# Attention in a hybrid decoder layer: the value products of two heads put side by side in the array, with transposed outputs

## The chip, the cores and the metric

The kernel runs on one core of one Trainium2 chip. The metric is the device time of one execution in microseconds (us). Engines are named as in the profile: PE (matrix multiply; PEld is its weight load), DVE (vector), ACT (scalar activations), POOL (GpSimd) and SP (issues most DMAs).

## The reference

One step of a one-layer hybrid decoder for a prompt of 1024 tokens behind 16 learned meta tokens (T = 1040 rows) and eight single-token samples, all in fp32. The layer has a state-space head group and a latent attention head group; both feed an output projection and a feed-forward part. The change touches only the causal attention of the prompt, with 8 heads, query and key width 96, value width 64, in query blocks of 128:

```python
s = jnp.einsum('bqhd,bkhd->bhqk', qb, kp).astype(jnp.float32) * ATTN_SCALE
s = jnp.where(kpos[None, :] <= qpos[:, None], s, -jnp.inf)
p = jax.nn.softmax(s, axis=-1)
return jnp.einsum('bhqk,bkhd->bqhd', p.astype(vp.dtype), vp)
```

The last einsum is the value product.

## The kernel before

The program is five blocks one after the other: the tiles block (projections, state-space scan, queries, keys, values into DRAM), the attention block (`attention_block`, this case), the samples block (paged attention of the eight samples), the mixing block and the feed-forward block. A block starts when every engine has finished the one before.

The attention block works on **units**. A unit is a query tile t of 128 rows with some of its heads: all 8 heads at t = 0, four at t = 1, two at t = 2 and 3, one from t = 4 on. Together 43 units, each head of which attends to t + 1 key blocks of 128. Two **tail units**, for the last 16 rows of four heads each, stand at places 39 and 43, so K = 45. All engines walk n from 0 up in the same order, written out by hand:

- PE, at step n: `turn(n - 2)` transposes the probabilities of unit n - 2 block by block into PSUM banks 6 (first half of the blocks) and 7 (second half) (L1216); `scores(n)` multiplies queries and keys into three PSUM banks, 0 to 2 or 3 to 5 by the parity of n (L1188, tail units L1200); `values(n - 2)` multiplies (L1228, tail units L1235).
- DVE, at step n: `copy_first(n - 2)` copies bank 6 into SBUF (`pt[0]`, L1119), `maximum(n)` adds the mask (L1106), takes the row maximum (L1113) and scales it (L1114); after the last unit of a tile, `finish` divides the tile's output by the row sums (L1133, L1134).
- ACT, at step n: `copy_second(n - 2)` copies bank 7 into `pt[1]` (L1166), `exps(n)` computes the exponentials with their row sums, one instruction for each head (L1155, tail units L1159).
- SP loads k, q and v tile by tile (L1059 to L1061), then the pages of the first two samples for the next block, then stores the attention output (L1068, L1073).

In `values`, the transposed probabilities (128 keys x 128 queries) are the weights of the matmul and 64 columns of v stream past them; the output has the queries on the 128 partitions and 64 columns for a head. All heads of a tile gather in one bank, 2 or 5 by the parity of t:

```python
ins = pe.matmul(ps[:, o_bank(t), h * VD:(h + 1) * VD], pt[g][:, c, :], v[:, b, h * VD:(h + 1) * VD],
                start=(b == 0), stop=(b == t))
```

One fp32 `matmul` of the program is two pairs of LDWEIGHTS and MATMUL in the trace, which the rows call records; a fp32 transpose is one pair. So 288 matmuls of `values` are 576 records. The tail units put four heads side by side, each in its own 32 columns of the array, at partitions 0, 32, 64 and 96 of the output (L1200, L1235); the samples block does the same at L1796 and L1799.

Of the kernel before, what the change touches and what calls it, by code (L numbers as in the profile page):

```python
# [24 lines left out]
ALU = mybir.AluOpType  # L25
# [944 lines left out]
def attention_block(nc, s, pages):  # L970
# [19 lines left out]
    done_order = sorted([(last_unit[t], t) for t in range(NT)] + [(n, NT) for n in tails])  # L990
# [7 lines left out]
    pt = [sb(f"pt{i}", [P, 4, P]) for i in range(2)]  # L998
# [11 lines left out]
    loaded = [sem(f"loaded{t}") for t in range(6)]  # L1010
    load_of = [0, 1, 2, 3, 4] + [5] * (NT - 4)
    loads = [3 * 16 * load_of.count(i) for i in range(6)]
# [4 lines left out]
    o_ready, att_done, att_stored = sem("o_ready"), sem("att_done"), sem("att_stored")  # L1017
    dve_steps = Steps(sem("dve_steps"), "attention dve")
    pool_steps = Steps(sem("pool_steps"), "attention pool")
    block = ctx.enter_context(nc.Block())  # L1020

    def o_bank(t):
        return 2 if t % 2 else 5

    TAIL_BANK = 5
# [14 lines left out]
    def outputs(n):  # L1040

        return [m for m, _ in done_order].index(n) + 1
# [8 lines left out]
    def output_done(n):  # L1051
        return is_tail(n) or n == last_unit[units[n][0]]
# [25 lines left out]
    def _(pool):  # L1078
# [4 lines left out]
        pool.affine_select(out=mask[:, :], in_=mask[:, :], compare_op=ALU.is_ge, fill=NEG,  # L1083
                           base=0, pattern=[[-1, P]], channel_multiplier=1).then_inc(consts, 1)
# [9 lines left out]
    def _(dve):  # L1094
# [21 lines left out]
        def copy_first(n):  # L1116
            dve.wait_ge(turned[0], first_turns(n))
            w = len(blocks_of(n)[0]) * P if not is_tail(n) else 4 * P
            dve.tensor_copy(pt[0][:, :, :].rearrange("p b r -> p (b r)")[:, 0:w], ps[:, 6, 0:w]).then_inc(copied[0], 1)  # L1119
# [5 lines left out]
        def finish(n):  # L1125
            dve.wait_ge(o_ready, n + 1)
            if not is_tail(n):
                t = units[n][0]
                l, o, dst = lsum[t][:, :], by_head(ps[:, o_bank(t), :], VD), by_head(att[:, t, :], VD)
            else:  # L1130
                u = tails.index(n)
                l, o, dst = ltail[:, u:u + 1], ps[:, TAIL_BANK, VD:2 * VD].unsqueeze(1), atail[:, u:u + 1, :]
# [1368 lines left out]
```

## Time and profile before

| | us |
|---|---|
| median of 3 runs | 2163.18 (2162.9 to 2163.27) |
| profiled execution, its own time | 2163.01 |
| span of the profiled execution | 2161.3 |
| attention block on PE, first scores to last value product | 477.4 to 653.5 |
| PE busy over the span | 2010.4 (93%) |
| DVE busy | 1192.9 (55%) |
| ACT busy | 624.0 (29%) |
| POOL busy | 634.9 (29%) |

The profile is one execution. Starts are counted in us from the start of the span. The duration of a matmul record holds its way through the pipeline, so records that follow each other overlap in time; what a stream costs is read from the distance between starts. In rows that merge several records, the first number is the start of the first one and x is their count.

### The profile page before, as it was taken

The page shows a single profiled execution, that of the slowest core. Times are in us where ns is not written, and L with a number is a line of the kernel's source. Part 1 is how long each engine was busy: PE and PEld are TensorE (multiplying, and loading weights), DVE is VectorE, ACT ScalarE, POOL GpSimd, SP SyncE. Part 2 cuts the span into 40 slices and gives each one's busy share as a digit, 9 for nine tenths or more (in the row PEclk, how much of TensorE's full clock was granted, in tenths as well). Part 3 has the DMA queues.
Part 4 walks back from the last instruction along what each step waited for, and adds up shares of the span by engine and source line. Part 5 has one row for each costly group of instructions (what it writes and reads, how often), then busy time and mean ns, then how long its engine had stood idle before and what let it go on. Part 6 is the DMA issues. An engine that isn't in the chain of part 4 may idle for free. (4 is left out here: it accounts for less than half of the span.)

```text
span 2161.3 us, 35037 instructions
## 1 busy us (share of the span) xinstructions
PE 2010.4 (93%) x12543; PEld 1636.4 (76%) x12543; DVE 1192.9 (55%) x1992; ACT 624.0 (29%) x1292; POOL 634.9 (29%) x586
## 2 busy tenths in 40 slices
PE   8999999759997999999999659799999999999998
PEld 4566666438876777777777438699999999999997
DVE  4567666736653766665666435354444444544444
ACT  2233332224433444443545222121111111211110
POOL 1334344330003533333323133242232322333211
PEclk9999999869997999999999879899999999999999
DMA  5111111147411012322223051212210122102201
GB/s 219 21 38 37 37 42 37 47 97 160 105 48 38 20 29 67 84 72 68 59 70 90 12 186 39 59 40 59 59 40 20 56 58 58 39 19 58 58 19 79
DMA packets 180683, 132.00 MB, mean 61 GB/s; under 512 B 61757, under 2 KB 165486, under 8 KB 180438
## 3 DMA queue, kind: packets, MB, share of 16 engines
q1 hardware_dynamic: 177190, 129.37, 21.1%
q0 software_dynamic: 144, 1.08, 0.2%
q8 instruction: 71, 1.16, 0.2%
q10 hardware_dynamic: 3232, 0.01, 0.1%
q14 instruction: 46, 0.38, 0.1%
HBM read 110.81 MB, written 19.65 MB: 60 GB/s over the span
## 5 line engine op out<-in xcount | busy, mean ns | idle before, releaser
L2399 PE MATMUL f_ps<-nT_hi,f_gu_hi 128*128 128x344 f32 x1056 | 338.3, 320 | 6.7 <-POOL f_gu_lo L2271 6.7
L2399 PE MATMUL f_ps<-nT_hi,f_gu_lo 128*128 128x344 f32 x1056 | 337.7, 320 | 0.0
L2399 PE MATMUL f_ps<-nT_lo,f_gu_hi 128*128 128x344 f32 x1056 | 337.4, 320 | 0.0
L1507 POOL TENSOR_TENSOR s_b_latT<-s_b_latT_hi,s_b_latT_lo 128x1024 f32<-128x1024 f32 x64 | 153.5, 2399 | 348.8 <-DVE s_b_latT_lo L1561 348.8
L1628 DVE TENSOR_REDUCE s_b_ssq<-s_b_ksq 128x8 f32<-128x512 f32 x256 | 172.8, 685 | 120.1 <-ACT s_b_ksq L1426 118.0
L1426 ACT ACTIVATE s_b_ksq<-s_ps 128x512 f32<-128x512 f32 x256 | 153.6, 600 | 215.5 <-PE s_ps L1779 171.6
L1779 PE MATMUL s_ps<-s_b_wk_hi,s_b_latT_hi 128*128 128x512 f32 x512 | 208.2, 407 | 7.0 <-ACT s_b_ksq L1426 7.0
L2399 PEld LDWEIGHTS f_ps<-nT_hi,f_gu_hi 128*128 128x128 f32 x1056 | 199.1, 189 | 7.5 <-POOL f_gu_lo L2271 7.1
L1779 PE MATMUL s_ps<-s_b_wk_lo,s_b_latT_hi 128*128 128x512 f32 x512 | 201.5, 394 | 0.0
L1779 PE MATMUL s_ps<-s_b_wk_hi,s_b_latT_lo 128*128 128x512 f32 x512 | 201.2, 393 | 0.0
L2399 PEld LDWEIGHTS f_ps<-nT_hi,f_gu_lo 128*128 128x128 f32 x1056 | 199.0, 188 | 0.0
L2399 PEld LDWEIGHTS f_ps<-nT_lo,f_gu_hi 128*128 128x128 f32 x1056 | 198.6, 188 | 0.4
L2361 DVE TENSOR_TENSOR h<-f_ps,h 128x1024 f32<-128x1024 f32 x88 | 107.8, 1225 | 144.2 <-PE f_ps L2428 144.2
L2372 DVE TENSOR_SCALAR f_e<-f_e 128x344 f32<-128x344 f32 x66 | 26.0, 394 | 239.2 <-ACT f_e L2327 239.2
L2373 DVE RECIPROCAL f_e<-f_e 128x344 f32<-128x344 f32 x66 | 152.0, 2303 | 2.2
L2286 POOL TENSOR_TENSOR f_hid_lo<-f_e,f_hid_hi 128x344 fp32r<-128x344 f32 x66 | 61.6, 933 | 281.4 <-ACT f_hid_hi L2335 281.4
L2428 PE MATMUL f_ps<-f_wd_hi,f_hid_hi 128*128 128x512 f32 x352 | 139.6, 397 | 0.2 <-issue 0.2
L2428 PE MATMUL f_ps<-f_wd_hi,f_hid_lo 128*128 128x512 f32 x352 | 138.7, 394 | 0.0
L2428 PE MATMUL f_ps<-f_wd_lo,f_hid_hi 128*128 128x512 f32 x352 | 138.7, 394 | 0.0
L2271 POOL TENSOR_TENSOR f_gu_lo<-gu_raw,f_gu_hi 128x1024 fp32r<-128x1024 f32 x44 | 105.7, 2423 | 87.1 <-ACT f_gu_hi L2312 86.6
L768 PE MATMUL t_ps<-t_w_in,t_xT 128*128 128x512 f32 (+2 forms) x384 | 130.8, 497 | 0.0
L1779 PEld LDWEIGHTS s_ps<-s_b_wk_hi,s_b_latT_hi 128*128 128x128 f32 x512 | 97.4, 190 | 29.4 <-ACT s_b_ksq L1426 10.0
(367 smaller groups left out, 3615.2 us busy)
## 6 DMA issues: line engine op xcount, KB each, us to landing
p_latn<-in_cache_kv_latent SPq DMA_DIRECT2D x256, 128.0 KB, 2.0
gu_raw<-in_w_gate SPq DMA_DIRECT2D x22, 512.0 KB, 4.0
gu_raw<-in_w_up SPq DMA_DIRECT2D x22, 512.0 KB, 5.4
f_wd_raw<-in_w_down SPq DMA_DIRECT2D x11, 1024.0 KB, 5.0
t_w_in<-in_w_in SPq DMA_DIRECT2D x8, 980.0 KB, 13.3
t_x<-in_x_prompt SPq DMA_DIRECT2D x8, 512.0 KB, 5.6
p_krn<-in_cache_k_rope SPq DMA_DIRECT2D x256, 16.0 KB, 1.8
h<-in_w_out SPq DMA_DIRECT2D x8, 512.0 KB, 9.0
```

Source lines behind the costliest of these rows:

```text
L768: ins = pe.matmul(dst, l, r, start=(n == 0), stop=(n == len(lhsT) - 1))
L1426: out(act.activation(ksq[j % 2][:, :], ps[:, 3 + j % 2, :], ACT.Square, scale=QK ** -0.5), "sq_done")
L1507: out(pool.tensor_tensor(out=flat(latT), in0=flat(latT_hi).bitcast(F32), in1=flat(latT_lo).bitcast(F32), op=ALU.add), "sum_done")
L1628: out(dve.tensor_reduce(ssq[p][:, GP * g + j, :], by_head(ksq[j % 2][:, :], NOPE), AXX, ALU.add), "red_done")
L1779: ins = pe.matmul(ps[:, 3 + j % 2, :], l[g % 2][:, c, j, :], w[:, c, :], start=(c == 0 and l is latT_hi and w is wk_hi), stop=(c == 1 and ...
L2271: out(pool.tensor_tensor(out=gu_lo[p][:, j, :, :], in0=gu_raw[:, j, :, :], in1=gu_hi[p][:, j, :, :].bitcast(F32), op=ALU.subtract), "gu_lo ...
L2286: out(pool.tensor_tensor(out=hid_lo[q][:, fi, cols], in0=e[c][:, :], in1=hid_hi[q][:, fi, cols].bitcast(F32), op=ALU.subtract), "hid_lo_done")
L2361: out(dve.tensor_tensor(out=rows_, in0=ps[0:R, bank:bank + 2, :], in1=rows_, op=ALU.add), "h_added")
L2372: dve_steps(dve, dve.tensor_scalar(e[c][:, :], e[c][:, :], 1.0, None, ALU.add))
L2373: dve_steps(dve, dve.reciprocal(e[c][:, :], e[c][:, :]))
L2399: ins = pe.matmul(ps[:, bank + j, 0:W], w[fi][:, j, k, :], x[:, k, cols], start=(k == 0 and w is gu_hi and x is nT_hi), stop=(k == KD - 1 ...
L2428: ins = pe.matmul(ps[0:R, bank + c, :], x[q][:, fi, col:col + R], w[:, fi, cols], start=(fi == 0 and w is wd_hi and x is hid_hi), stop=(fi ...
```

## The change

The value product is turned round. The 64 columns of v of one head become the weights, the transposed probabilities (128 columns) stream past them, and the output has the value dimension on the partitions and the queries in the free dimension. Two heads share the array: the even one in columns 0 to 63 (output partitions 0 to 63), the odd one in columns 64 to 127 (partitions 64 to 127); their matmuls are issued in turn, key block by key block, each after a wait for the copy of its block.

- Units are gathered into **jobs**: up to t = 3 a unit is a job; from t = 4 on two successive units (two heads) are one. There are 27 jobs: 1, 2, 4, 4, and four for each of t = 4 to 7. `values(j)` runs on PE at the step of the job's last unit + 2, after `scores(n)`, into bank 2, whatever the tile. It waits until ACT has read the job before out of that bank.
- ACT copies the turned output of the job from bank 2 to SBUF (`keep_turned_output`, one of four buffers `oT`), at the start of its step last + 3, ahead of `copy_second` and `exps`.
- PE turns it back, one 128 x 128 transpose for each head pair (32 in all), at step last + 5, between `turn` and `scores`, into bank 5 (`back`).
- DVE divides by the row sums for each job, no longer for each tile, from bank 5, at step last + 5, ahead of `maximum`.
- `pt` has three slots for each half: two for the units of a job and one for the tail units.
- The tail units keep their products in 32-column groups, now into bank 2. A tail unit's scores still wait for bank 5 to be free, now on the division of the last job turned back, which at both tail units is that of the same step.
- The loads of tiles 3 and 4 share a semaphore, and PE waits for the identity matrix instead of for the mask (not shown).

```diff
-    done_order = sorted([(last_unit[t], t) for t in range(NT)] + [(n, NT) for n in tails])
+    jobs = []
+    for t in range(NT):
+        own = [n for n in range(K) if units[n][0] == t]
+        step = 1 if len(units[own[0]][1]) > 1 else 2
+        jobs += [own[i:i + step] for i in range(0, len(own), step)]
+    ending = {job[-1]: j for j, job in enumerate(jobs)}
+    BACK = 5
+    done_order = sorted([(job[-1] + BACK, job[-1]) for job in jobs] + [(n + 3, n) for n in tails])
...
-    pt = [sb(f"pt{i}", [P, 4, P]) for i in range(2)]
+    pt = [[sb(f"pt{i}{j}", [P, 4, P]) for j in range(3)] for i in range(2)]
+    oT = [sb(f"oT{i}", [P, H // 2, P]) for i in range(4)]
...
-    load_of = [0, 1, 2, 3, 4] + [5] * (NT - 4)
...
+    load_of = [0, 1, 2, 3, 3] + [4] * (NT - 4)
...
-    def o_bank(t):
-        return 2 if t % 2 else 5
...
+    O_BANK, BACK_BANK = 2, 5
...
+    def pt_slot(n):
+
+        if is_tail(n):
+            return 2
+        return [job.index(n) for job in jobs if n in job][0]
...
+        def finish(j):
+            t, heads = units[jobs[j][0]][0], heads_of(j)
+            l = lsum[t][:, heads[0]:heads[0] + len(heads)]
             dve_steps(dve, dve.reciprocal(l, l))
-            dve.tensor_tensor(out=dst, in0=o, in1=bc(l, VD, 2), op=ALU.mult).then_inc(att_done, 1)
-
-        dve.wait_ge(consts, 2)
-        for n in range(K + 3):
+            dve.wait_ge(back_ready, j + 1)
+            cols = slice(heads[0] * VD, (heads[-1] + 1) * VD)
+            dve.tensor_tensor(out=by_head(att[:, t, cols], VD), in0=by_head(ps[:, BACK_BANK, 0:len(heads) * VD], VD),
+                              in1=bc(l, VD, 2), op=ALU.mult).then_inc(att_done, 1)
+
+        def finish_tail(n):
+            u = tails.index(n)
+            l = ltail[:, u:u + 1]
+            dve_steps(dve, dve.reciprocal(l, l))
+            dve.wait_ge(o_ready, outputs_before(n) + 1)
+            dve.tensor_scalar(atail[:, u, :], ps[:, O_BANK, 0:VD], l, None, ALU.mult).then_inc(att_done, 1)
...
+        for n in range(K + BACK):
             if 2 <= n < K + 2:
                 copy_first(n - 2)
+            if n - 3 in tails:
+                finish_tail(n - 3)
+            if n - BACK in ending:
+                finish(ending[n - BACK])
             if n < K:
                 maximum(n)
             if n - 2 in tails:
                 copy_last(n - 2)
-            if n >= 3 and output_done(n - 3):
-                finish(n - 3)
...
+        def keep_turned_output(j):
+            w = len(heads_of(j)) // 2
+            act.wait_ge(o_ready, outputs_before(jobs[j][-1]) + 1)
+            if j >= 4:
+                act.wait_ge(back_ready, j - 3)
+            act.activation(oT[j % 4][:, 0:w, :], ps[:, O_BANK, 0:w * P].rearrange("p (w r) -> p w r", r=P),
+                           ACT.Copy).then_inc(oT_copied, 1)
+
+        for n in range(K + 3):
+            if n - 3 in ending:
+                keep_turned_output(ending[n - 3])
+            if 2 <= n < K + 2:
                 copy_second(n - 2)
             if n < K:
...
-                pe.wait_ge(att_done, outputs(tails[u - 1] if u else last_unit[NT - 2]))
+                backs = [job[-1] for job in jobs if job[-1] + BACK <= n]
+                pe.wait_ge(att_done, outputs(backs[-1]))
...
+        def values(j):
+            if j >= 1:
+                pe.wait_ge(oT_copied, j)
+            for m in tails:
+                if m + 2 < jobs[j][-1] + 2 and (j == 0 or jobs[j - 1][-1] < m):
+                    pe.wait_ge(att_done, outputs(m))
+            for w in range(len(heads_of(j)) // 2):
+                pair = heads_of(j)[2 * w:2 * w + 2]
+                blocks = {h: [] for h in pair}
+                for n in jobs[j]:
+                    for g in range(2):
+                        for c, (i, h, b) in enumerate(blocks_of(n)[g]):
+                            if h in pair:
+                                blocks[h].append((n, g, c))
+                t = units[jobs[j][0]][0]
+                for b in range(t + 1):
+                    for i, h in enumerate(pair):
+                        n, g, c = blocks[h][b]
+                        pe.wait_ge(copied[g], first_turns(n) if g == 0 else n + 1)
+                        ins = pe.matmul(ps[i * VD:(i + 1) * VD, O_BANK, w * P:(w + 1) * P], v[:, b, h * VD:(h + 1) * VD],
+                                        pt[g][pt_slot(n)][:, c, :], start=(b == 0), stop=(b == t))
             ins.then_inc(o_ready, 1)
 
-        pe.wait_ge(consts, 1)
-        for n in range(K + 2):
-            if n >= 2:
+        def back(j):
+            pe.wait_ge(oT_copied, j + 1)
+            if j >= 1:
+                pe.wait_ge(att_done, outputs(jobs[j - 1][-1]))
+            for w in range(len(heads_of(j)) // 2):
+                ins = pe.transpose(ps[:, BACK_BANK, w * P:(w + 1) * P], oT[j % 4][:, w, :], ident[:, :])
+            ins.then_inc(back_ready, 1)
+
+        def tail_values(n):
+            u = tails.index(n)
+
+            pe.wait_ge(oT_copied, sum(job[-1] < n for job in jobs))
...
+        pe.wait_ge(consts, 2)
+        for n in range(K + BACK):
+            if 2 <= n < K + 2:
                 turn(n - 2)
+            if n - BACK in ending:
+                back(ending[n - BACK])
             if n < K:
                 scores(n)
-            if n >= 2:
-                values(n - 2)
+            if n - 2 in ending:
+                values(ending[n - 2])
+            if n - 2 in tails:
+                tail_values(n - 2)
```

`tail_values` goes on as the old tail branch did, into bank 2.

## Rows read from the trace of the kernel before

**Rows 1.** The page: the chain that ended last, by engine.
```profile
PE 35%; POOL 0%; issue 0%; DVE 0%; ACT 0%
```

**Rows 2.** Busy time of PE, PEld, DVE, ACT, POOL, 500 to 620 us, attention block.
```profile
500.00:620.00 120.00, 119.96 (x805) 96.83 (x804) 77.28 (x151) 50.05 (x117) 0.00 (x0) 1.00 0.43 111
```

**Rows 3.** PE in order of time, eight-block units (start us, us, engine, what).
```profile
613.59 1.90 PE L1228 MATMUL a_ps<-a_v,a_pt 128*128 128x64 f32 x16
615.32 1.04 PE L1216 MATMUL a_ps<-a_ident,a_prob 128*128 128x128 f32 x8
616.20 1.88 PE L1188 MATMUL a_ps<-a_k,a_q 96*128 96x512 f32 x4
617.92 1.90 PE L1228 MATMUL a_ps<-a_v,a_pt 128*128 128x64 f32 x16
```

**Rows 4.** PE in order of time, a six-block unit.
```profile
555.88 1.45 PE L1228 MATMUL a_ps<-a_v,a_pt 128*128 128x64 f32 x12
557.17 0.82 PE L1216 MATMUL a_ps<-a_ident,a_prob 128*128 128x128 f32 x6
557.83 1.46 PE L1188 MATMUL a_ps<-a_k,a_q 96*128 96x512 f32 x4
```

**Rows 5.** SP's queue: last stores of the attention output, first load after them.
```profile
616.40 38.39 SPq L1068 DMA_DIRECT2D s_att<-a_att  x2
654.83 3.67 SPq L1073 DMA_DIRECT2D s_att<-a_atail  x8
659.92 0.52 SPq L1346 DMA_DIRECT2D s_b_h<-in_state_ssm  x1
```

**Rows 6.** PE's groups by form, 477 to 654 us: the value matmuls.
```profile
L1228 PE MATMUL a_ps<-a_v,a_pt 128*128 128x64 f32 x576 | 69.7, 272 | 0.4 <-DVE a_pt L1119 0.3
```

**Rows 7.** PE in order of time in the samples block: 128, 32, 128 columns.
```profile
686.89 0.39 PE L1779 MATMUL s_ps<-s_b_wk_lo,s_b_latT_hi 128*128 128x512 f32 x1
687.12 0.39 PE L1779 MATMUL s_ps<-s_b_wk_hi,s_b_latT_lo 128*128 128x512 f32 x1
687.44 0.65 PE L1796 MATMUL s_ps<-s_b_latT,s_b_qab 128*32 128x128 f32 x16
687.90 0.40 PE L1799 MATMUL s_ps<-s_b_krT,s_b_qab 128*32 128x128 f32 x8
688.23 1.09 PE L1730 MATMUL s_ps<-s_b_ident,p_latn 128*128 128x128 f32 x8
689.16 0.27 PE L1733 MATMUL s_ps<-s_b_ident,p_krn 128*128 128x128 f32 x1
```

**Rows 8.** PE in order of time, a tail unit: matmuls in 32-column groups.
```profile
631.50 1.10 PE L1235 MATMUL a_ps<-a_v,a_pt 128*32 128x64 f32 x64
633.48 0.31 PE L1235 MATMUL a_ps<-a_v,a_ptl 16*32 16x64 f32 x8 [0.88 <-DVE a_ptl L1123]
```

**Rows 9.** ACT's groups by form in the block, and a 128-wide copy of the next.
```profile
L1166 ACT ACTIVATE a_pt<-a_ps 128x512 f32<-128x512 f32 x17 | 10.1, 594 | 2.8 <-PE a_ps L1216 2.8
L1166 ACT ACTIVATE a_pt<-a_ps 128x384 f32<-128x384 f32 x20 | 9.7, 483 | 0.0
L1155 ACT ACTIVATE a_prob<-a_ps,a_nmx 128x1024 f32<-128x1024 f32 x8 | 8.9, 1116 | 21.4 <-DVE a_nmx L1114 21.4
...
688.37 0.28 ACT L1428 ACTIVATE s_b_scs<-s_ps 128x128 f32<-128x128 f32 x1 [0.22 <-PE s_ps L1799]
```

**Rows 10.** DVE's groups by form in the block: division and reciprocal.
```profile
L1134 DVE TENSOR_TENSOR a_att<-a_ps,a_lsum 128x512 f32<-128x512 f32 x8 | 5.5, 692 | 0.3
...
L1133 DVE RECIPROCAL a_lsum<-a_lsum 128x8 f32<-128x8 f32 x8 | 1.6, 195 | 1.8 <-PE a_ps L1228 1.8
```

**Rows 11.** DVE, then ACT, in order of time, beside the unit of rows 4.
```profile
556.08 0.30 DVE L1106 TENSOR_TENSOR a_ps<-a_ps,a_mask 128x128 f32<-128x128 f32 x1 [1.06 <-PE a_ps L1188]
556.42 0.96 DVE L1113 TENSOR_REDUCE a_mx<-a_ps 128x1 f32<-128x768 f32 x1
...
557.60 0.90 ACT L1155 ACTIVATE a_prob<-a_ps,a_nmx 128x768 f32<-128x768 f32 x1 [1.64 <-DVE a_nmx L1114]
```

More of the change, by code:

```diff
@@ L1008, in attention_block @@
     ident = sb("ident", [P, P])
-    loaded = [sem(f"loaded{t}") for t in range(6)]
-    load_of = [0, 1, 2, 3, 4] + [5] * (NT - 4)
-    loads = [3 * 16 * load_of.count(i) for i in range(6)]
+    loaded = [sem(f"loaded{t}") for t in range(5)]
+    load_of = [0, 1, 2, 3, 3] + [4] * (NT - 4)
+    loads = [3 * 16 * load_of.count(i) for i in range(5)]
     consts, scores_ready, max_ready, exp_done = [
@@ L1017, in attention_block, with heads_of @@
     o_ready, att_done, att_stored = sem("o_ready"), sem("att_done"), sem("att_stored")
+    oT_copied, back_ready = sem("oT_copied"), sem("back_ready")
     dve_steps = Steps(sem("dve_steps"), "attention dve")
-    pool_steps = Steps(sem("pool_steps"), "attention pool")
+    pool_steps = Steps(consts, "attention constants")
     block = ctx.enter_context(nc.Block())
-    def o_bank(t):
-        return 2 if t % 2 else 5
-    TAIL_BANK = 5
+    O_BANK, BACK_BANK = 2, 5
+    def heads_of(j):
+        return [h for n in jobs[j] for h in units[n][1]]
+    def pt_slot(n):
+        if is_tail(n):
+            return 2
+        return [job.index(n) for job in jobs if n in job][0]
     def places(n):
@@ L1040, in outputs, with outputs_before @@
     def outputs(n):
-        return [m for m, _ in done_order].index(n) + 1
+        return [m for _, m in done_order].index(n) + 1
+    def outputs_before(n):
+        return sum(job[-1] < n for job in jobs) + sum(m < n for m in tails)
     def first_turns(n):
@@ L1049, in is_tail @@
         return units[n][0] == NT
-    def output_done(n):
-        return is_tail(n) or n == last_unit[units[n][0]]
     @block.sync
@@ L1082, in _ @@
         pool_steps(pool, pool.memset(mask[:, :], 0.0))
-        pool.affine_select(out=mask[:, :], in_=mask[:, :], compare_op=ALU.is_ge, fill=NEG,
-                           base=0, pattern=[[-1, P]], channel_multiplier=1).then_inc(consts, 1)
+        pool_steps(pool, pool.affine_select(out=mask[:, :], in_=mask[:, :], compare_op=ALU.is_ge, fill=NEG,
+                                            base=0, pattern=[[-1, P]], channel_multiplier=1))
         pool_steps(pool, pool.memset(tmask[:, :], 0.0))
@@ new lines, in back, with weigh @@
+        def back(j):
[8 more added lines that the diff above has]
+            pe.wait_ge(oT_copied, sum(job[-1] < n for job in jobs))
+            def weigh(b, w, src):
+                for i in range(HT):
+                    h = u * HT + i
+                    ins = pe.matmul(ps[i * QT:(i + 1) * QT, O_BANK, 0:VD], src[0:w, i * QT:(i + 1) * QT],
+                                    v[0:w, b, h * VD:(h + 1) * VD], start=(b == 0), stop=(b == NT))
+                return ins
+            pe.wait_ge(copied[0], first_turns(n))
+            pe.transpose(ps[0:META, 6, 0:P], prob[n % 2][:, SEQ:T], ident[:, :]).then_inc(turned[0], 1)
+            for b in range(4):
+                weigh(b, P, pt[0][2][:, b, :])
+            pe.wait_ge(copied[1], n + 1)
+            for b in range(4):
+                weigh(4 + b, P, pt[1][2][:, b, :])
+            pe.wait_ge(copied[0], first_turns(n) + 1)
+            weigh(NT, META, ptl).then_inc(o_ready, 1)
```

43 lines of the change are left out of this document (3 added, 40 removed).

## The prediction

> **What bounds the kernel now.** I read the page first. Its chain that ended last lies on PE for the part it reaches back over [rows 1], and that part is the feed-forward block, which the change leaves alone. So the question is whether the attention block ends sooner, and whether what follows moves with it. The busy table of the block's steady part comes next: PE 119.96 of 120 us, DVE 77, ACT 50, at a granted clock of 1.00, that is 2.4 GHz [rows 2]. PE has no gap to fill; time leaves here only if PE is given less to do, and only as long as DVE and ACT still arrive in time. PE's order of time then gives the price of each piece by the distance between starts: for eight key blocks, values 1.73 us (16 records), transposes 0.88, scores 1.72, period 4.33 [rows 3]; for six, values 1.29 and transposes 0.66 [rows 4], with scores of 6 x 0.215 a period of 3.24. So a key block of one head costs 0.216 of values, 0.11 of transposes and 0.215 of scores.
>
> At the end of the block SP issues the last small stores, and 1.4 us after the last of them the next block's first load starts [rows 5]. Since a block starts when the one before is done, a shorter attention block should pass its gain on whole. The page loads for the next block are in SP's queue ahead of the stores; a store that stands behind them goes out at 616.40 [rows 5], 37 us before the block's end, so they cost nothing up to a gain of that size.
>
> **What goes.** 576 records of values [rows 6], two for each of 288 matmuls: 288 x 0.216 = 62.2 us. A record streams only 64 columns but loads 128 columns of weights, and its distance of 0.108 is the same as that of a transpose with 128 columns and 128 weights (0.11) [rows 3]. The weights set the old price.
>
> **What comes in its place.** 288 matmuls that stream 128 columns past 64 weight columns, two at a time if the column groups overlap. The trace has no two 64-column groups side by side. The nearest rows have four 32-column groups. In the samples block 16 records of 128 columns take 0.46 us from start to the next line's start: four waves of four, 0.115 each [rows 7]. In the tail unit 64 records of 64 columns last 1.10 us with the pipeline's own 0.2 us in it [rows 8], which is 16 waves at 0.055. So groups side by side cost what one costs. At two groups I take 0.22 us for both heads' matmuls of one key block (two records each): 144 x 0.22 = 31.7 us, a gain of 30.5. Bounds: both groups one after the other, 63.4 us (a loss of 1.2); less than 31.7 can't be, as 128 columns of an fp32 record have no shorter distance in any row.
>
> The Trainium skill (TensorE: Matmul & The Clock Gate, Packing small matmuls) gives a measured 2.38x for three column groups. At that efficiency, by an estimate from its figure, two groups would give 1.59x, the new products 40 us, and the forecast would be some 8 us later. The 64 records of the tail unit speak against it: a full fourfold rate.
>
> **Switches of column width.** Before the 32-column records of rows 7 the distance is 0.32 instead of 0.23; behind them, the last two waves and the way out take 0.33 instead of 0.22, and the eight transposes after that 0.93 instead of 0.88. Together 0.09 + 0.11 + 0.05 = 0.25 us for going in and out. 27 jobs: 6.8 us. Bounds 0 and 13. The Trainium skill (TensorEngine Tiling, Key Properties) says a change of tiling mode drains the engine; the 0.25 us is this trace's size of it, and the page gives none.
>
> **Turning back.** 32 transposes at 0.11: 3.5 us on PE. ACT gets 27 copies, 24 of them 128 wide at 0.28 us [rows 9], about 8 us on an engine that is busy 42% of the time [rows 2]. DVE's 8 divisions of 512 columns with their reciprocals, 7.1 us [rows 10], become 27 smaller ones at about 0.5 (0.2 + the 0.3 that 128 columns take in rows 11), 13 us, on an engine that is busy 64%. Neither becomes the busiest. The semaphore that tiles 3 and 4 now share and the wait for the identity matrix cost nothing: PE runs without a gap from 500 us on, and all loads of both tiles were needed soon after in any case. The 288 waits ahead of single matmuls are for copies mostly long done; one in the middle of the value stream of rows 3 leaves the 16 records at 1.73 us, so I take zero, bound 288 x 0.01 = 3.
>
> **PE's sum:** -62.2 + 31.7 + 6.8 + 3.5 = **-20.2 us**, -4.0 of it up to t = 3 and -16.2 from t = 4 on.
>
> **The waits that come.** PE's slack was what covered DVE and ACT, and the products now come in one lump every second unit. Take t = 5, counted from the end of a unit's scores (555.88 in rows 4). DVE's mask and maximum and ACT's exponential follow; ACT starts it at 557.60 and is free 0.90 later [rows 11]; only then it can do `copy_second` of the unit before, 0.48 [rows 9]: 3.10 us, 3.15 with the semaphore. PE in the new order has transposes 0.66, the next scores 1.29, the way in 0.09, and seven matmuls (0.77) before it needs the second half of that unit: 2.81. It stands for about 0.35 us a pair. The same count gives 0.3 at t = 4. For eight blocks the exponential takes 1.12, the copy 0.59 [rows 9] and DVE at most 0.3 more (0.96 us for 768 columns), 3.8 us, against 0.88 + 1.72 + 0.09 + 0.99 = 3.68: 0.1 or less, and so at t = 6. Per pair, old to new with the wait: t = 4, 5.41 to 5.0; t = 5, 6.48 to 5.93; t = 6, 7.57 to 6.5; t = 7, 8.66 to 7.37. Four pairs each: -13.2 us.
>
> Up to t = 3 every unit is a job. `values` of the next one waits until ACT has emptied bank 2, and ACT does that behind two or more exponentials of the unit between: about 1.7 (DVE) + 1.2 + 0.28 = 3.2 us against 2.85 of PE work, and `copy_second` stands behind it. I take 0.3 for each of 11 jobs, 3.2 us; bounds 0 and the whole 4.0. What is left is -0.8.
>
> The tail units break the rhythm. Unit 43's scores wait for a division of the same step, which stands in DVE's queue behind the maximum of unit 42 (2.0 from the end of its scores: the 1.7 of rows 11 and 0.3), a copy (0.6, as on ACT) and its own 0.5: 3.1 us where PE arrives after 1.0, so 2.1; at unit 39 values lie between, 0.5. Unit 43's own products wait for a copy that DVE does behind the maximum of unit 44: 2.6 against 0.9, so 1.7, then 0.5 for ACT's half; the last job waits 0.5 for the tail's division, and the last transpose back 0.4 for ACT's copy. 5.7 us; bounds 2 and 9.
>
> **Sum:** -13.2 - 0.8 + 5.7 = -8.3, or -20.2 + 3.0 + 3.2 + 5.7. From the profiled execution's own 2163.0 (span 2161.3 and 1.7 around it) this is 2154.7; the median of the runs is 0.2 higher. Some waits overlap with the drain of a switch (PE stands anyway), so I say **2154.5**.
>
> **Rivals.**
> (1) *The two groups run one after the other* (slower). Place: `values`, where each matmul begins with a wait, and both passes of one head are issued before the other head's. If the other group can't start until they are through, the products cost 63.4 us instead of 62.2; with 3.5 and 6.8 and some 4 of waits (less, as PE is late itself) it is +15: **2178**. It decides at a price of 0.17 us a matmul: from there on the change loses. For: no row has two 64-column groups with a wait on each matmul. Against: the tail units issue both passes of one head, then the next, and reach the fourfold rate [rows 8]. Chance 0.09.
> (2) *The waits are hidden or small*, and the PE sum is nearly had: -15 to -20, **2146**. For: ACT and DVE are half idle. Against: the counts above are in order and leave no slack at t = 4, 5 and at the tails. Chance 0.14.
> (3) *Emptying PSUM becomes the limit.* ACT now has three jobs in a fixed order, and a late one delays `copy_second`, hence the next transposes, hence the next exponentials. If this costs 0.5 us more at each of the 16 pairs, nothing is left: **2163**. Against: at t = 7 ACT has about 2.0 us of work a unit and DVE 2.7, PE 3.6. Chance 0.09. The Trainium skill (TensorEngine Tiling, PSUM Bottleneck) states it as a rule: tiling speeds up the matmuls, not the copies.
> (4) *Forecast case*, 2148 to 2161: chance 0.68.
>
> **Numbers.** About 0.2% (4.3 us) can be told from no change. Faster by more: the forecast case up to 2159, and (2): 0.83. Within: 0.08, from (3) and the forecast's upper edge. Slower: (1), 0.09. The range 2147 to 2161 leaves out (1), half of (3) and a part of (2).
>
> **What the profile would show.** Right: MATMUL records of `values` of form 128*64 with 128 columns, starting in pairs, 16 key blocks of a pair's two heads in about 1.8 us instead of 3.5; the block ending near 645 instead of 653.5; PE idle before `values` on ACT's `pt`, and a gap of about 2 us before the second tail's scores; busy PE in 500 to 600 no longer full. Wrong: 3.5 us for the 16 (rival 1); no idle time on PE in the block (rival 2); a period of 8.6 us for two eight-block units with PE idle a sixth of it (rival 3); or the next block's start not moving with the end of attention, which no row of before excludes.

## The result and the profile after

| | before | after |
|---|---|---|
| time, median of 5 runs each, same chip | 2163.18 us (2161.58 to 2163.86) | 2172.83 us (2171.12 to 2174.62) |
| ratio after / before | | 1.0046, 95% interval 1.0031 to 1.0060 |
| profiled execution: span, own time | 2161.3, 2163.0 us | 2169.2, 2171.12 us |

The changed kernel is slower, by 9.65 us. The forecast was 2154.5 us and faster. Of all runs below one was slow, one of e6's ten with 7369.55 us, and its ratio leaves it out. The page of the changed kernel first: its totals, two of its DMA queues and the chain by engine.

```profile
PE 2000.2 (92%) x12575; PEld 1608.6 (74%) x12575; DVE 1197.6 (55%) x2030; ACT 630.0 (29%) x1319; POOL 633.8 (29%) x586
...
q8 instruction: 107, 1.75, 0.3%
...
q14 instruction: 67, 0.55, 0.1%
...
PE 35%; issue 0%; DVE 0%; POOL 0%; ACT 0%; DVEq 0%
```

The chain is still PE's [rows 1]. What a reader passes over easily are the two queues named "instruction": they bring code. In the page of before they had 71 and 46 packets.

**Where the time went** is read from the first PE instruction of each block. PE in order of time (start us, us, engine, what), before:

```profile
477.44 0.77 PE L1188 MATMUL a_ps<-a_k,a_q 96*128 96x128 f32 x2 [14.96 <-DMA a_v<-s_v]
664.58 0.64 PE L1712 MATMUL s_ps<-s_b_ident,p_wk 128*64 128x128 f32 x2 [11.12 <-POOL s_b_ones L1492]
1241.05 0.56 PE L2132 MATMUL m_ps<-m_ident,gu_raw 8*128 8x8 f32 x4 [7.36 <-DMA gu_raw<-s_att]
1396.33 0.65 PE L2399 MATMUL f_ps<-nT_hi,f_gu_hi 128*128 128x344 f32 x1 [6.68 <-POOL f_gu_lo L2271]
```

and after:

```profile
474.43 0.98 PE L1222 MATMUL a_ps<-a_k,a_q 96*128 96x128 f32 x3 [14.52 <-DMA a_v<-s_v]
657.47 0.85 PE L1773 MATMUL s_ps<-s_b_ident,p_wk 128*64 128x128 f32 x3 [10.57 <-POOL s_b_ones L1553]
1240.58 0.56 PE L2193 MATMUL m_ps<-m_ident,gu_raw 8*128 8x8 f32 x4 [8.50 <-DMA gu_raw<-s_att]
1396.61 0.66 PE L2460 MATMUL f_ps<-nT_hi,f_gu_hi 128*128 128x344 f32 x1 [6.68 <-POOL f_gu_lo L2332]
```

The differences of such rows give one line for each kernel. The last column runs to the start of PE's last instruction; 3.0 us of the first column are chance, since the tiles block is the same code in all of them (its ends scatter from 474.4 to 478.1 where nothing is put in front of attention).

| kernel | start of attention | attention | samples | mixing | feed-forward |
|---|---|---|---|---|---|
| before | 477.4 | 187.1 | 576.5 | 155.3 | 760.2 |
| after | 474.4 | 183.0 | 583.1 | 156.0 | 767.9 |
| e1: after, PE's code moved back | 486.9 | 181.4 | 573.5 | 156.1 | 760.8 |
| e2: after, ACT's moved back | 477.5 | 181.8 | 580.4 | 156.3 | 768.0 |
| e3: after, all moved back | 487.4 | 182.0 | 572.8 | 154.9 | 760.2 |
| e4: before, code moved as in after | 485.0 | 187.2 | 584.0 | 156.4 | 768.3 |
| e5: after, hidden padding | 476.8 | 181.5 | 577.2 | 156.0 | 760.8 |
| e8: e5 with the wait filled | 477.0 | 179.9 | 578.9 | 156.1 | 760.7 |
| e9: e8, all in the old places | 477.4 | 186.2 | 574.5 | 154.9 | 760.2 |
| e10: before, 56 more on PE | 477.2 | 187.3 | 577.2 | 156.6 | 760.9 |
| e11: before, 64 more | 476.1 | 187.2 | 574.0 | 156.3 | 760.9 |
| e14: before, 88 more | 478.1 | 189.2 | 575.2 | 156.8 | 765.5 |
| e13: before, 112 more | 477.0 | 191.9 | 579.6 | 156.3 | 767.9 |

Each line is one execution. Attention did get shorter: 187.1 to 183.0 us, and 181.4 to 182.0 in e1, e2, e3 and e5, which repeat it. Then 6.6 us are lost in the samples block, 0.7 in mixing and 7.7 in feed-forward, blocks in which the change edits nothing.

The chain of waits in the feed-forward block, 1560 to 1740 us, shows where. Before it is PE alone; after, once in each pass of the loop (every 139 us), PE stands. Before, then after (start us, us, what):

```profile
1560.00 43.36 PE f_ps L2399 x276
1603.36 0.99 PE f_ps L2410 x8
```

```profile
1559.88 21.69 PE f_ps L2460 x138
...
1581.66 0.53 DVE f_e L2437
1582.19 0.37 issue
1582.56 2.45 PE f_ps L2460 x14
1585.01 0.30 issue
1585.31 20.57 PE f_ps L2460 x130
```

PE's waits of the changed kernel, 1400 to 2150 us (us in total, times, longest), have two entries that before lacks:

```profile
PE f_ps L2460 <- DVE f_e L2437: 4.3, 4, 1.2
PE f_ps L2460 <- issue: 1.1, 4, 0.3
```

5.4 of the 7.7 us stand there, four times 1.35. Division (DVE) is charged although it had been done as early as in before; "issue" is the better name. By the distance from one jump back to the next, each of the four passes takes 1.6 to 2.0 us more (137.4 before, 139.0 to 139.3 after), 7.1 us together. The DMA view from 1580 to 2120 us says what PE lacks. Before, then after (queue, kind: packets, MB, share):

```profile
q1 hardware_dynamic: 31296, 23.07, 14.8%
```

```profile
q1 hardware_dynamic: 31296, 23.07, 14.9%
q8 instruction: 34, 0.56, 0.4%
```

Same data, and 34 packets of code of 16 KB that before doesn't fetch: there PE's loop is fetched once and stays. Such a packet holds 256 instructions: between the first and the last of ten fetches inside attention, the trace of before has 2306 records of PE, weight loads and waits included. Counted like this the change adds 112 records on PE, 50 on ACT and 67 on DVE, all in attention, so every later loop moves. By the compiled programs PE's feed-forward loop (1614 instructions) moves from 118 to 230 behind a border of 256.

The samples block has the same sign. PE's waits in it, before, then after:

```profile
PE s_ps L1730 <- issue: 6.4, 2, 3.3
```

```profile
PE s_ps L1791 <- issue: 10.8, 4, 3.4
...
PE s_ps L1791 <- DMA p_krn<-in_cache_k_rope: 2.8, 3, 1.1
```

The four kernels that have PE's code in the changed place (after, e2, e4, e13) stand 9.7 to 10.8 us on "issue" there, in four pieces; all others 6.2 to 6.9 us in two.

**Inside attention** the rows that answer to rows 2 to 4 and 8. Busy time by engine, 500 to 620 us and from there to 654 (which holds 7 us behind attention's end), as in rows 2:

```profile
500.00:620.00 120.00, 118.85 (x894) 80.45 (x893) 84.16 (x193) 58.92 (x148) 0.00 (x0) 1.00 0.39 102
620.00:654.00 34.00, 21.28 (x286) 15.31 (x284) 12.14 (x29) 9.23 (x16) 0.75 (x5) 0.85 0.03 10
```

PE in order of time, six-block units (rows 4 before), eight-block units and the tails:

```profile
553.98 1.97 PE L1273 MATMUL a_ps<-a_pt,a_v 128*64 128x128 f32 x24
555.88 0.88 PE L1251 MATMUL a_ps<-a_ident,a_prob 128*128 128x128 f32 x6
556.59 0.27 PE L1282 MATMUL a_ps<-a_ident,a_oT 128*128 128x128 f32 x1
...
560.03 1.97 PE L1273 MATMUL a_ps<-a_pt,a_v 128*64 128x128 f32 x24
...
606.87 2.13 PE L1273 MATMUL a_ps<-a_pt,a_v 128*64 128x128 f32 x32
608.93 1.09 PE L1251 MATMUL a_ps<-a_ident,a_prob 128*128 128x128 f32 x8
...
610.86 1.97 PE L1235 MATMUL a_ps<-a_k,a_q 96*32 96x512 f32 x24 [0.73 <-DVE a_att L1148]
...
628.33 2.31 PE L1235 MATMUL a_ps<-a_k,a_q 96*32 96x512 f32 x24 [1.94 <-DVE a_att L1148]
630.57 3.24 PE L1273 MATMUL a_ps<-a_pt,a_v 128*64 128x128 f32 x32
...
639.09 0.27 PE L1298 MATMUL a_ps<-a_ident,a_prob 128*16 128x128 f32 x1 [1.65 <-DVE a_pt L1136]
...
640.12 1.08 PE L1293 MATMUL a_ps<-a_v,a_pt 128*32 128x64 f32 x32 [0.18 <-ACT a_pt L1190]
...
641.50 1.97 PE L1251 MATMUL a_ps<-a_ident,a_prob 128*128 128x128 f32 x8
...
644.23 1.97 PE L1273 MATMUL a_ps<-a_pt,a_v 128*64 128x128 f32 x32 [0.59 <-issue]
646.57 0.33 PE L1282 MATMUL a_ps<-a_ident,a_oT 128*128 128x128 f32 x1 [0.37 <-ACT a_oT L1197]
```

Eight key blocks of two heads take 2.06 us from start to the next line's start (606.87 to 608.93) instead of twice 1.73 [rows 3]: the two column groups do work side by side. The same 32 records take 3.24 at 630.57, behind the longest wait. The eight transposes at 641.50 are slow too, 1.97 us instead of 1.09 at 608.93: from 641 to 643 us the granted clock is 0.50 in this execution.

### The profile page after: what moved, and what is told of

Its sections match the earlier page's. It is cut to its first block and busy times, and to the rows that moved or that the text cites. A ratio compares the mean times of both kernels' runs of the same rounds, so it can differ in the third digit from the quotient of the medians.

```text
span 2169.2 us, 35266 instructions
## 1 busy us (share of the span) xinstructions
PE 2000.2 (92%) x12575; PEld 1608.6 (74%) x12575; DVE 1197.6 (55%) x2030; ACT 630.0 (29%) x1319; POOL 633.8 (29%) x586
## 3 DMA queue, kind: packets, MB, share of 16 engines
q0 software_dynamic: 144, 1.08, 0.2%
## 5 line engine op out<-in xcount | busy, mean ns | idle before, releaser
L1622 DVE TENSOR_TENSOR s_b_latT_lo<-s_ps,s_b_latT_hi 128x512 fp32r<-128x512 f32 x128 | 82.6, 685 | 67.6 <-ACT s_b_latT_hi L1469 67.4
```

Source lines behind the costliest of these rows:

```text
L1622: out(dve.tensor_tensor(out=latT_lo[g % 2][:, :, 2 * bank:2 * bank + 2, :], in0=ps[:, bank, :].rearrange("p (c j t) -> p c j t", c=2, t=P) ...
```

## The experiments

Moving code needs instructions that do nothing. Two waits on a met semaphore become one instruction. In the first set they stand where the engine waits for attention's first data. Each set ran on a chip of its own with before beside it, so sets are compared by their ratios.

### First set: is it the place of the code?

```diff
-        pe.wait_ge(consts, 2)
+        for _ in range(289):            # e1, e3: 144 instructions on PE
+            pe.wait_ge(consts, 2)
+        for _ in range(156):            # e2, e3: 78 on ACT
+            act.wait_ge(consts, 2)
+        for _ in range(123):            # e3: 61 on DVE
+            dve.wait_ge(consts, 6)
```

(e4 has 112, 50 and 67 such instructions in the kernel before.)

**e1_after_pe.** 

> The changed kernel with 144 more instructions on PE that do nothing (waits that are already met), put where PE waits for attention's first load; they move PE's later code to the place modulo 256 instructions that it had before. Theory A (code placement: PE's feed-forward loop of 1614 instructions now lies over 8 blocks of 256 instead of 7 and is fetched again in each of its passes): the feed-forward block takes 761.9 us again instead of 769.5, the fetches of PE's queue stop inside the loop, and the kernel takes 2172.8 - 7.6 = 2165 us; the samples block stays at 563 us. Theory B (the loss behind attention comes from data: the clock, DMA traffic or SBUF places of the later blocks): no change, 2173 or slower.

**e2_after_act.** 

 Theory A (code placement): the samples block takes 555.5 us again instead of 563.3, kernel 2165 us; the feed-forward block stays at 769.5. Theory B: no change, 2173. Rival within A: the samples block's loss is due to PE's or DVE's code, then ACT's alone changes nothing, and the first kernel or the third of this set shows it.

**e3_after_all.** 

> The changed kernel with do-nothing instructions on PE (144), ACT (78) and DVE (61), so that all code behind attention lies as in the kernel before, modulo the block size of its engine. Theory A: the gain of attention comes through: 2172.8 - 7.6 - 7.8 and up to 1.9 for the mixing block = 2155.5 to 2157.5 us, which is the forecast's 2154.5 within its rounding. Theory B: 2173. If only part of the loss is placement: between.

**e4_before_all.** 

> The kernel before, its attention untouched, with do-nothing instructions in attention's head on PE (112), ACT (50) and DVE (67), which put all later code where the changed kernel has it. Theory A: it is slower by what the changed kernel lost behind attention, 7.6 + 7.8 and up to 1.9: 2178.5 to 2180.5 us, with the fetches inside the feed-forward loop as in the changed kernel. Theory B: no change, 2163.

| | median us | ratio to before (2161.99, 21 runs) |
|---|---|---|
| e1 | 2165.48 | 1.0012 (1.0003 to 1.0022) |
| e2 | 2169.33 | 1.0035 (1.0023 to 1.0048) |
| e3 | 2164.02 | 1.0012 (1.0002 to 1.0022) |
| e4 | 2184.39 | 1.0102 (1.0085 to 1.0118) |

The expectations took the blocks between other marks (samples 555.5 and 563.3, feed-forward 761.9 and 769.5 us); what counts in them is the difference.

Theory B falls: e4 has the attention of before and loses 22.4 us, 14.9 without the padding's own 7.5. Theory A holds by the blocks. With PE's code moved back (e1, e3) feed-forward takes 760.8 and 760.2 us; with ACT's alone (e2) it stays at 768.0. The samples block surprised: PE's place gives back 9.6 us (e1), ACT's alone 2.7 (e2), so the 7.8 that I had put on ACT belong mostly to PE, and e2's total missed its 2165. The totals of e3 and e4 missed because the padding was not free: attention starts 10.0 and 7.5 us later than in before. Taken off, e3 is at 2154 and e4 at 2177. That e1's total met its forecast of 2165 is luck: 9.5 us of padding (its attention starts at 486.9) hide what the samples block gave back. What one such instruction costs is seen in e1 (count, duration in ns, first and last start in us):

```profile
L1308 PEldq EVENT_SEMAPHORE  x144: 51/51/51, 471.2 to 486.7; - x144
```

They start 0.108 us apart, 15.5 us in all. In before PE waits 6.4 us for the data at this place; in e1 the padding runs over the same wait, so only the rest shows.

### Second set: padding that hides, and what is left in attention

e5 puts 52 instructions on PE behind attention's last transposes back, and 42 on ACT at the old place. e6 to e8 are e5 with one edit each:

```diff
+        for _ in range(104):            # e5, behind the loop over units
+            pe.wait_ge(oT_copied, 1)
@@ e6
-                        pe.wait_ge(copied[g], first_turns(n) if g == 0 else n + 1)
+                        need = first_turns(n) if g == 0 else n + 1
+                        if need > waited[g]:
+                            pe.wait_ge(copied[g], need)
+                            waited[g] = need
@@ e7
-            if n - 3 in ending:
-                keep_turned_output(ending[n - 3])
             if 2 <= n < K + 2:
                 copy_second(n - 2)
+            if n - 3 in ending:
+                keep_turned_output(ending[n - 3])
@@ e8, in scores() of the second tail unit, ahead of its wait for DVE
+                    for _ in range(16):
+                        pe.transpose(flat[:, lo:lo + P], ident[:, :], ident[:, :])
```

**e5_pads_hidden.** 

> The changed kernel with 52 do-nothing instructions on PE behind its last transposes back, where PE stands 11 us before the next block, and 42 on ACT in attention's head. Theory A (code placement, and the padding at PE's head cost its own 10 us in the first set): nothing is paid for the padding, attention's own gain of some 5 us is left whole: 2172.8 - 7.7 (feed-forward) - 9 (samples, as the first kernel of the first set) = 2156 us, with attention up to the next block's first PE instruction at 182 us. Rival (PE's samples loop needs the very place it had before): the samples block stays above 580 us and the kernel at 2162 to 2165.

**e6_fewer_waits.** 

> The kernel with the hidden padding, and the values' wait ahead of each single matmul kept only where the awaited value rises (the instructions and their places are the same, only the waits go). The forecast priced the 288 waits at zero, bound 3 us. If zero holds: the PE span of attention is unchanged (170.9 us within 0.3). If each costs 0.01 us: 2 to 3 us less.

**e7_copy_first.** 

> The kernel with the hidden padding, and ACT copies the second half of a unit's turned probabilities before it keeps a job's turned output, instead of after. If ACT's order is what makes PE stand within the jobs (0.23 to 0.31 us at the record 14 of the jobs of five and six key blocks): those gaps shrink by up to the copy's 0.28, some 2 us in all. If the exponential ahead of the copy sets it, as the forecast said: unchanged within 0.5 us; and the next job's start may come later, since its wait for the kept output is then served later.

**e8_fill_wait.** 

> The kernel with the hidden padding, and 16 transposes of the identity matrix (the region is written over by the scores behind them) in front of the last tail unit's wait, so that PE works in the 1.9 us in which it stood there; padding behind is shortened by as many instructions. Theory C (the granted clock fell from 2.4 to 1.2 GHz because PE stood still at the second tail unit, and the 24 scores and 32 products behind it paid 0.54 and 1.08 us): the granted clock stays at 1.00 there, the products take 1.97 instead of 3.05 us, attention ends 1.6 us sooner. Rival (the clock falls for another reason, or the transposes delay the scores by themselves): no gain, or up to 0.5 us lost.

| | median us | ratio to before (2162.05, 26 runs) | PE, first to last of attention |
|---|---|---|---|
| e5 | 2158.51 | 0.9979 (0.9970 to 0.9989) | 170.7 us |
| e6 | 2158.90 | 0.9983 (0.9973 to 0.9993) | 171.0 |
| e7 | 2158.47 | 0.9977 (0.9966 to 0.9989) | 171.5 |
| e8 | 2158.65 | 0.9976 (0.9965 to 0.9987) | 169.0 |

e5 beats both kernels: the same arithmetic as the changed kernel, some 14 us less, for nothing but places. It is 2.5 us above my 2156; the samples block took 577.2 where e1 had 573.5, and 2.2 of these 3.7 us are waits for a load of `p_krn` that e1 doesn't have. e6: the waits ahead of single matmuls cost nothing that can be seen. e7: ACT's order isn't what stops PE in the jobs of six blocks; the copy waits behind the exponential either way. In e5 ACT's exponential starts at 555.53 and the copy directly behind it at 556.43 for 0.48 us, and PE's next record starts at 556.96; in e7 the copy starts at 557.66 and PE's record at 558.19. The 0.8 us that e7 takes more on PE lie at the block's start, where its granted clock stays low for longer (0.50 from 491 to 495 us, 0.93 in e5). e8 shows the clock. PE in order of time at the second tail unit and the 20 us around it (the last columns are granted clock, DMA share, GB/s), e5:

```profile
630.19 2.51 PE L1237 MATMUL a_ps<-a_k,a_q 96*32 96x512 f32 x24 [1.94 <-DVE a_att L1148]
632.64 3.05 PE L1275 MATMUL a_ps<-a_pt,a_v 128*64 128x128 f32 x32
...
632.00:634.00 2.00, 2.00 (x26) 1.64 (x20) 1.22 (x2) 0.00 (x0) 0.00 (x0) 0.50 0.00 0
620.00:640.00 20.00, 16.48 (x179) 10.89 (x177) 10.33 (x22) 6.71 (x14) 0.00 (x0) 0.91 0.00 1
```

and e8:

```profile
628.31 1.91 PE L1233 MATMUL a_ps<-a_ident 128*128 128x128 f32 x16
630.32 1.97 PE L1240 MATMUL a_ps<-a_k,a_q 96*32 96x512 f32 x24
632.22 1.97 PE L1278 MATMUL a_ps<-a_pt,a_v 128*64 128x128 f32 x32
...
620.00:640.00 20.00, 17.36 (x222) 11.85 (x224) 11.38 (x25) 7.95 (x17) 0.00 (x0) 1.00 0.00 1
```

In e5 PE stands 1.94 us, the granted clock falls from 2.4 to 1.2 GHz (0.50 from 632 to 634 us; 0.91 is the mean over 20 us), and scores and products behind it take 0.54 and 1.08 us longer. With PE kept at work over the same wait the clock stays at 1.00, the two lines take 1.97 each, and attention is 1.7 us shorter, here and in e9, which has the same filling (168.8). Not every stand does it: PE also waits 1.65 us before 640.95 in e5, and the clock stays at 1.00. The total doesn't show the gain: the samples block of e8's profiled execution is 1.7 longer, and the medians of e5 and e8 differ by 0.14 us. Where the 1.7 us go stays open.

### Third set: old places, the border, and the order of the heads

```diff
@@ e9: e8 with 112 instructions on PE behind attention, 78 on ACT and 61 on DVE at its head
@@ e10, e11 (and e13, e14): before, behind the loop over units; 2 x 56, 2 x 64, 2 x 112, 2 x 88
+        for _ in range(2 * 56):
+            pe.wait_ge(consts, 1)
@@ e12: e5 with
-                for b in range(t + 1):
-                    for i, h in enumerate(pair):
+                for i, h in enumerate(pair):
+                    for b in range(t + 1):
```

**e9_old_places.** 

> The changed kernel with the 16 filling transposes at the second tail unit and do-nothing instructions on PE (112, behind attention's last transposes back), ACT (78) and DVE (61), so that all code behind attention lies where the kernel before has it, modulo the block size, and the padding hides. Theory A (placement) with theory C (clock): attention 179.9 us as in the kernel with the filled wait, samples 573 to 576.5, mixing 155, feed-forward 760.3: 2155 to 2157 us. Rival (a shorter attention block is partly given back by the samples block itself, as its first pages came 0.9 us nearer to those of the kernel before without any code moved): 2158 as with the two kernels with hidden padding.

**e10_before_56.** 

> The kernel before with 56 do-nothing instructions on PE behind attention's last values, where PE stands 11 us. The feed-forward loop (1614 instructions) then begins 175 behind a border of 256 and ends 3 instructions ahead of one: 7 blocks. Theory A: the feed-forward block stays at 760.3 us and is fetched once; the samples block may change by a few us, since its loop moves too. Rival (any moved code costs, by distance, not by the count of blocks): the feed-forward block takes longer here already.

**e11_before_64.** 

> The same with 64 instead of 56: the feed-forward loop begins at 183 and reaches 5 instructions into an eighth block. Theory A: the feed-forward block takes 768 us, with fetches in each pass, for 8 instructions that do nothing; the samples block as in the kernel with 56 within 1 us; so 7 to 8 us slower than that one. Rival: no difference from the kernel with 56 that can be measured.

**e12_head_by_head.** 

> The changed kernel with the hidden padding of the second set, and in the values all products of one head issued before those of the other (same instructions, same columns of the array, other order). If the two column groups work side by side only because their products stand next to each other in the queue: the 32 records of a job of eight key blocks take 3.5 to 3.9 us instead of 1.97, attention is 27 us longer or more in PE's sum (144 x 0.22 = 31.7 us twice instead of once, less the waits that this hides), kernel some 2185 us: this is what the forecast's first rival would have cost. If the array looks further ahead: unchanged, 2158.5.

e9: 2160.14 us, ratio to before (2163.25, 29 runs) 0.9984 (0.9974 to 0.9994). A miss by my padding again. From PE's last instruction of attention to the next block's first it took 17.4 us where e5 takes 10.9. Without those 6.5 it stands at 2153.6, and samples, mixing and feed-forward are at the values of before or below. That this can be had in one kernel isn't shown.

e10 and e11: 2165.12 and 2164.63 us, ratios 1.0004 and 1.0006, both intervals with 1. e11 was to pay 7 to 8 us and pays nothing, so touching an eighth block is not the border. (Behind attention the trace counts one instruction more than asked for in each of these kernels, 57, 65, 89 and 113 in e10, e11, e14 and e13; the loop's places in the expectations include it.)

e12: 2171.65 us in its one run, 13 above e5. Groups of PE in attention (busy us, mean ns), e5, then e12:

```profile
L1275 PE MATMUL a_ps<-a_pt,a_v 128*64 128x128 f32 x576 | 44.1, 285 | 2.8 <-ACT a_oT L1197 1.6 <-issue 1.1
```

```profile
L1275 PE MATMUL a_ps<-a_pt,a_v 128*64 128x128 f32 x576 | 59.1, 284 | 0.5 <-issue 0.5
```

and a job of eight key blocks in e12:

```profile
616.29 3.33 PE L1275 MATMUL a_ps<-a_pt,a_v 128*64 128x128 f32 x32
```

Same records, same columns of the array, 15 us more for another order: the groups overlap only where their matmuls alternate in the queue. In e5 the two heads' records start in pairs, 0.006 to 0.033 us apart and 0.109 from pair to pair; in e12 they start one by one, 0.109 apart. My +27 was too much, and the 3.33 us lie below my 3.5 to 3.9, for two reasons. PE's waits (2.8 to 0.5 us here, and those between the records of a job) vanish when PE is later. And at the change from one head to the other some records still run side by side: 28 records take 2.82 us to the next line's start and not 3.05. The forecast's rival 1, 23.5 us above it, had the same faults, if less.

### Fourth set: PE's place alone, and the border again

**e13_before_112.** 

> The kernel before with 112 do-nothing instructions on PE behind attention's last values and nothing else: PE's later code alone lies where the changed kernel has it (the feed-forward loop 231 behind a border of 256). Theory A with PE alone: feed-forward 768 us with 107 fetches on PE's queue instead of 71, samples 580 to 584 us, mixing 156.3: 2163 + 7.6 + 4 to 7, and 0 to 6.5 for padding that is not hidden here (112 such instructions at this place lengthened the way to the next block by 6.5 us in an earlier run): 2175 to 2184 us. Rival (ACT's and DVE's places are needed for it too): the samples block stays at 574 to 577.

**e14_before_88.** 

> The same with 88: the loop begins at 207 and reaches 29 instructions into an eighth block. With 64 it reached 5 into it and was still fetched once only, so the count of blocks that it touches does not set the border by itself. Theory A2 (the loop is lost when PE asks for a ninth block behind the eighth, before it jumps back, and that needs more than a few instructions of the eighth): feed-forward 768 us already here. If the border lies further in: 761 us, and only the kernel with 112 pays.

e13: 2179.67 us, ratio to before (2162.93, 9 runs) 1.0080 (1.0063 to 1.0097). e14: 2170.10, ratio 1.0033 (1.0020 to 1.0046), between the two answers that I had written down. DMA from 1580 to 2120 us, e11 (64), then e14 (88):

```profile
q1 hardware_dynamic: 31296, 23.07, 15.0%
```

```profile
q1 hardware_dynamic: 31296, 23.07, 15.0%
q8 instruction: 35, 0.57, 0.4%
```

With PE's instructions alone moved, the kernel before pays 7.7 us in feed-forward and the code queue of the other engines stays at 46 packets. The border lies between 64 and 88: at 64 the loop reaches 5 instructions into its eighth block and no ninth is fetched; at 88, 29 instructions in, PE fetches on in every pass and pays 4.6 us; at 112, 53 in, 7.0 (against the 760.9 of e10 and e11). The traces have nine fetches in each pass for both; at 88 PE stands once a pass, at 112 twice. In the changed kernel the ninth fetch since the block's start is issued at 1575.1 us, 7 us before the first pause above; e11 has eight. That a fetch running ahead of the loop's end pushes out its beginning fits all of this; that it is the mechanism is argued, not shown.

The Trainium skill (Runtime: NRT & Kernel Launch, Instruction fetch mechanics) says that a taken branch whose target isn't in the window of fetched pages stalls the engine for a fetch, and that PE's instruction memory holds 2048 instructions. The rows agree with the first: the pauses come once a pass, just behind the jump back. They don't speak against the second: 1614 instructions stay, eight blocks of 256 would be 2048, and the loops that pay are those that ask for a ninth. The same section calls the memory two lines with a window of two pages; here seven blocks stay resident (in e11 eight), so the rows differ from it.

The padding behind attention is hidden up to 64 instructions (attention 187.2), then costs 2.1 us at 88 and 4.7 at 112; the step between them is 24 times 0.108. The samples block with PE's code in the changed kernel's place: 579.6 (e13), 580.4 (e2), and 583.1 (after) and 584.0 (e4) where ACT's is there too; in all others 572.8 to 578.9. PE's place costs 3 to 7 us there. ACT's seems to add some 3 to it, and none in e1, where PE's is back; these are single executions, and e5 and e8, whose code lies alike, are 1.7 apart.

## Why the prediction was wrong

**The step that failed** is the sentence after the price of a block: "Since a block starts when the one before is done, a shorter attention block should pass its gain on whole." The next block did start earlier, as said. But the sum counted what instructions cost where they stand, and nothing for what they push: 112 more on PE, 50 on ACT, 67 on DVE. That is worth 7.7 us in feed-forward (e13: PE alone), 6.6 in samples and 0.7 in mixing, 15.0 in all and nearly three times what attention gains. No rival had it, and my last sign of being wrong (the next block's start not moving) looked at the wrong place. The 7.7 us are shown by e1, e3 and e13; that the 6.6 are PE's code too rests on the pauses named above. The queues of code stood on the page of before; how near the longest loops were to the size that stays was not asked.

**The PE sum** (-20.2) is had in records: side by side at 0.11 us for a pair of records, one of either head. The products of eight key blocks take 2.06 us (606.87 to 608.93) where 8 x 0.22 and the 0.25 of the switch give 2.01. What lies around it is larger than I took. In the six-block jobs a pair of units takes 6.05 us (553.98 to 560.03), forecast 5.93; the wait for `copy_second` in it was right in cause: the copy starts directly behind ACT's exponential, and e7's other order leaves it there.

**The waits ahead of single matmuls**, taken as zero: in e6 nothing of them can be seen.

**The tails**, 5.7 us in six terms: 0.73 and 1.94 (forecast 0.5 and 2.1) for DVE's division, 1.65 (1.7) for the copy, 0.18 (0.5) for ACT's half, 0.59 (0.5) before the last job, 0.37 (0.4) before the last transpose. The count of what stands in DVE's queue gave each within 0.35 us in this execution. The 0.59 is partly luck: the slow transposes at 641.50 took up a part of that wait, and in e5, where they are fast, it is 1.07. What the count lacked is that the 1.94 us of standing have a second price, 1.6 us of the lower clock behind them; in the changed kernel's own execution the clock fell a second time at the tail (641.50), for about 1 us more.

**Attention in all**: -8.3 forecast, -3.6 on PE in the changed kernel's execution (175.7 to 172.1, with the second fall of the clock and a later rise at the block's start), -5.1 in e5 (to 170.7), -6.8 in e8. So 1.7 of the 3.2 us that e5 is short of were the clock's. Some 1.0 of the rest lies in the jobs up to t = 3, which were to gain 0.8: from attention's first scores to those of the first unit of t = 4 it takes 51.4 us before and 51.6 in e5. From there to the first scores of t = 7, it takes 79.0 and 71.3 us, 7.7 less where the forecast's three sets of four pairs had 8.1.

**Rivals.** (1) is refuted by 606.87 and priced by e12: 13 to 15 us more, not 23.5. (2) by the waits. (3): PE is busy 118.85 of 120 us, so emptying PSUM is no limit. The forecast's number itself was near what the change is worth where its code lies as before (e3 and e9 less their padding, 2154, that is 8 and 10 us under before), and that is a number worked out, not a run.

## What to carry to other kernels

An edit of an early stage moves the code of every later one. Before pricing an unrolled edit, look at the instruction queues of the page, count the instructions that it adds to each engine, and see which later loops are near the size that stays resident; measure such a change with padding that holds the later places, and look for a place where that padding hides. A wait newly put on a full PE costs its own length and, where the granted clock falls, the slow stretch behind it; filling it with work of no use took 1.7 us off the block (e8), though not off the kernel's median.

## What the runs showed of the hardware

- 24 instructions that do nothing, 88 instead of 64, cost 4.6 us in a block that starts some 750 us later (e11 and e14: 760.9 and 765.5 us; in the medians, 2164.63 and 2170.10 us of two sets, padding that no longer hides is 2.0 of the difference).
- Do-nothing instructions on PE start 0.108 us apart (e1: 144 of them from 471.2 to 486.7 us). At the head of a block the 6.4 us in which PE waits for a load anyway hide a part, and 10.0 us show.
- Column groups of 64 worked side by side at full rate when their matmuls alternated in the queue and, but for the change of heads, one after the other when they didn't (e5 and e12: 44.1 and 59.1 us).
- A stand of 1.94 us on PE brought the granted clock down to 1.2 GHz, and 16 transposes in it kept it at 2.4 (e5, e8); a stand of 1.65 us some 10 us later left it at 2.4 in e5, and in the changed kernel's own execution a second fall followed it.
